# A hybrid decoder layer on one core: three raw weight buffers instead of two, seven slots of split weights instead of five, and the gates' row operations spread over more products

## The chip, the cores and the metric

The kernel runs on one core of one Trainium2 chip. The metric is the device time of one execution in microseconds (us). The time before is 2606.9 us, the median of three runs (2606.17 to 2619.28).

## The reference, cut to what matters

One layer is applied to 2048 prompt tokens and to 8 x 4 sample tokens, with D = 1024 and a feed-forward width of 2816, all in float32.

```
a = rmsnorm(x, g_mix);  u = a @ w_in            # q, k, v, gates, o, B, C, h
C_t = f_t C_{t-1} + i_t k_t v_t^T               # mLSTM, chunkwise, 4 heads
h = o * headnorm(q^T C / max(|q.n|, 1));  y = B * conv3(C * h)
x += concat(h, y) @ w_out
x += (silu(f @ w_gate) * (f @ w_up)) @ w_down   # f = rmsnorm(x, g_ffn)
x += sigmoid(x @ w_pg) * rmsnorm(p @ w_ple, g_ple)
y = rmsnorm(x, g_final)
```

The gates' rows are scalars for each head and token: log forget gates are summed within a chunk (a scan), a running maximum is taken (a second scan), and differences of these rows are exponentiated.

## The kernel before, in words

The tokens go through in three groups ("supers") 0, 1 and 2 of 704, 704 and 672 tokens, and each super goes through the whole layer. A product of TensorE is 12 matmuls of 128x128 weights with half a super's tokens (352 or 336 columns): a float32 product is made of three fp32r ones, high*high, high*low and low*high (`three`, L606). A pair of 256 output columns is computed by seven such products instead of eight (Strassen's scheme, P1 to P7), so sums of weight quarters (S1 to S4) are needed as well as the quarters themselves.

**The way of a weight.** SP loads raw float32 weights of a pair into one of the two buffers wraw (`raw`, L1071; raw r waits until raw r-2 is used up). DVE makes the four sums of a pair (L1771 S1, L1779 S2, L1783 S3, L1787 S4), 128x512 elements each; S3 and S4 overwrite parts of the raw buffer. ACT rounds a quarter or sum to its high part (L1294), and POOL subtracts to get the low part (L2688). Both parts of one entry lie in a slot of the ring wring (5 slots); entry e takes the slot of entry e-5, once TensorE's product with that is done (L1280). In super 0 SP writes the split sums to memory (weight_parts, L1088). In supers 1 and 2 ACT's queue loads them back into the ring (L1286) instead of DVE, ACT and POOL making them again; only A12 and A22 are then split anew. Each wait on a kept or loaded part is on one of six semaphores in turn.

**The order** is written out by hand: every engine walks through the same list of products and calls its `ahead()` once a product. ACT and POOL thereby prepare the entry four products ahead of TensorE; DVE makes its sum five ahead. These distances are set by the calls before the loop (four on ACT and POOL, `AHEAD + 1` on DVE, L2587), by the calls inside the first pair of a super (`Plain.aheads`, L99: at four of the eight products), and by two calls behind it. Because an engine is in order, whatever a call waits for also holds up the eviction that stands behind it.

**DVE** also combines the products out of PSUM: in the later pairs it reads P6 (L1851, which frees the bank that TensorE's P7 needs), P7 (L1858, L1824), P2, P4 and P3 (L1827, L1829); in the first pairs and those with four banks L1840, L1847, L1849, L1824. Two "duos" (w_out 0 and 1; w_gate 0 and w_up 0) interleave the products of two pairs, so that they need two raw buffers at once; ahead of each, DVE makes the operands (differences of activations and their low parts, L1797, L2027 to L2035), with L1908 reading P6. In the feed-forward stage DVE also makes the low part of the hidden layer behind each up pair (L2427, two of 128x704).

**The gates** are computed behind the products numbered s = 8 to 28 of a super: DVE makes masks at s = 8, logs at 11, both scans at 13 (L2078, L2079), the sample's scans (super 2 only) and all differences at 15 (L2101 to L2112), and the parts at 17 (L2118 to L2120).

SP's loop goes by raw r: it issues raw r, then what is due there (reloads of x at r = 13 and 14, next tiles at 51 to 53), then keeps the parts of raw r-1.

Of the kernel before, what the change touches and what calls it, by code (L numbers as in the profile page):

```python
# [7 lines left out]
F32 = mybir.dt.float32  # L8
# [26 lines left out]
RING = 5  # L35
AHEAD = 4
# [62 lines left out]
BY_TOKENS = Plain(("a", "b", "P2", "P4", "c", "d", "P3", "P5"), (0, 1, 2, 6), (0, 5, 6, 7))  # L99
# [67 lines left out]
def build(nc, x_prompt, x_sample, p_prompt, p_sample, state_C, state_n, state_m, state_conv, g_mix, w_in,  # L167
# [37 lines left out]
    wraw = [at(f"wraw{p}", [P, 2048], F32, w0 + p * 8192) for p in range(2)]  # L205
    spare_raw = at("spare_raw", [P, 2048], F32, w0 + 20480 + RING * 4096 + 5632)
# [5 lines left out]

    mix0 = w0 + 20480 + RING * 4096
    expE = at("expE", [P, NH, P], F32, mix0)
# [73 lines left out]
    y_roots = keep("y_roots", [P, 3])  # L288
    assert cursor[0] <= nc.sbuf_usable_end, (cursor[0], nc.sbuf_usable_end)
# [29 lines left out]
    n_sums, n_prepared, n_landed = [0], [0], [0, 0]  # L319
# [3 lines left out]
    def add_raw(pieces):  # L323

        r = len(raws)
        raws.append(pieces)
        end[r] = 0
        n_landed[r % 2] += 16 * len(pieces)
        raw_landed.append(n_landed[r % 2])
        return r, wraw[r % 2]  # L330
# [176 lines left out]
    with ExitStack() as ctx:  # L507
# [7 lines left out]
        landed = [sem("landed_even"), sem("landed_odd")]  # L515
        parts_kept, parts_loaded = [sem(f"parts_kept{j}") for j in range(6)], [sem(f"parts_loaded{j}") for j in range(6)]
# [49 lines left out]
        def _(pe):  # L566
# [26 lines left out]
            def entry_ready(e):  # L593
                w = entries[e]
                if w.prepared:
                    pe.wait_ge(lo_done, w.prepared)
                else:
                    pe.wait_ge(parts_loaded[w.loads % 6], 16 * ((w.loads + 5) // 6))
# [469 lines left out]
        def _(sp):  # L1068
            n_raw = [0]

            def raw():  # L1071

                r = n_raw[0]
                n_raw[0] += 1
                if r >= len(raws):
                    return
                if r >= 2:
                    sp.wait_ge(lo_done, raw_end[r - 2])
                for where, src in raws[r]:
                    sp.dma_start(wraw[r % 2][:, where].rearrange("p (k n) -> p k n", k=src.shape[1]), src)\  # L1080
                        .then_inc(landed[r % 2], 16)

            def keep_parts(which, names=None):

                for e, w in enumerate(entries):
                    if w.raw in which and w.kept and (names is None or names(w)):
                        sp.wait_ge(lo_done, w.prepared)
                        sp.dma_start(weight_parts[w.kept - 1], wring[e % RING][:, :].bitcast(F32))\  # L1088
                            .then_inc(parts_kept[w.kept % 6], 16)
# [172 lines left out]
        def _(act):  # L1262
# [8 lines left out]
            def one_ahead():  # L1271
# [6 lines left out]
                if e >= RING:  # L1278
                    if entries[e - RING].spare is None:
                        act.wait_ge(prod, entry_end[e - RING])  # L1280
                    before = entries[e - RING].kept
                    if before:
                        act.wait_ge(parts_kept[before % 6], 16 * ((before + 5) // 6))
                if w.loaded:
                    act.wait_ge(parts_kept[w.loaded % 6], 16 * ((w.loaded + 5) // 6))
                    act.dma_start(wring[e % RING][:, :].bitcast(F32), weight_parts[w.loaded - 1])\  # L1286
                        .then_inc(parts_loaded[w.loads % 6], 16)
                    return
                if w.first:
                    act.wait_ge(landed[w.raw % 2], raw_landed[w.raw])  # L1290
# [438 lines left out]
        def _(dve):  # L1729
# [31 lines left out]
            def one_ahead():  # L1761
# [5 lines left out]
                for name, r, v, where, turn, first, second in sums_at.get(e, ()):  # L1767
                    if name == "S1":
                        dve.wait_ge(landed[r % 2], raw_landed[r])
# [305 lines left out]

            def gate_scans(q):
                T, TP, n = q.T, q.TP, q.nch
                link(nc.vector.tensor_tensor_scan(B[0:NH, 0:T], W[0:NH, 0:T], LF[0:NH, 0:T], 0.0, mul, add))  # L2078
# [19 lines left out]
            def gate_weights(q):  # L2098
                T, TP = q.T, q.TP
                dve.wait_ge(parts_clear, NTILE * (q.n + 1))  # L2100
                link(nc.vector.tensor_tensor(R1[0:NH, 0:T], B[0:NH, 0:T], M[0:NH, 0:T], sub))  # L2101
                link(nc.vector.tensor_tensor(CS[0:NH, 0:T], G[0:NH, 0:T], B[0:NH, 0:T], sub))
                whole = TP // P * P
# [153 lines left out]
            def in_after(q):  # L2257
                def after(s):
# [660 lines left out]
```

## Time and profile before

| | us |
|---|---|
| median of three runs | 2606.9 |
| lowest and highest | 2606.17, 2619.28 |
| span of the profiled execution | 2611.0 |
| TensorE (PE) busy | 2487.7 |
| VectorE (DVE) busy | 1491.2 |
| ScalarE (ACT) busy | 906.9 |
| GpSimd (POOL) busy | 1050.4 |

The span runs from the first to the last instruction of one profiled execution. Its own time outside the profile is not given; the span lies 4.1 us over the median of the runs. "Idle before" and a bracket such as `[6.14 <-DVE u L1858]` give how long the engine stood idle before the instruction and what ended that. PEclk is the granted clock of TensorE: 1.00 is 2.4 GHz and 0.50 is 1.2 GHz.

### The profile page before, as it was taken

To read this page: it belongs to the slowest core of one execution; us is meant where nothing else is said; L and a number is where in the kernel's file an instruction comes from. 1 tells how busy PE (TensorE), PEld (TensorE's weight loads), DVE (VectorE), ACT (ScalarE), POOL (GpSimd) and SP (SyncE) were. 2 spreads that over 40 slices of the span, in tenths; PEclk is the share of its full clock that TensorE was granted. 3 is DMA by queue.
4 is the path that set the end of the run, shared out by engine and by line. 5 is a ranking of instruction groups with operands and counts; after the bars stand their busy time and mean duration, and the time that the engine had idled before them with its cause. 6 is when DMAs were issued, how large, how long until landed. Compare 5 with 4: busy or idle time off the path is not lost.

```text
span 2611.0 us, 41191 instructions
## 1 busy us (share of the span) xinstructions
PE 2487.7 (95%) x15829; PEld 2430.8 (93%) x15829; DVE 1491.2 (57%) x2287; ACT 906.9 (35%) x1688; POOL 1050.4 (40%) x864
## 2 busy tenths in 40 slices
PE   8898888999999999999999999999999999999998
PEld 7898788999999998999999999998899999999997
DVE  7667887665555683466643333468357664333355
ACT  5344453343334543334322121354134432212133
POOL 5666655576666342222332122333223232312233
PEclk8999899999999999999999999999999999999999
DMA  5656635576566746575556545575557555565545
GB/s 187 211 176 227 219 134 186 185 275 225 207 229 226 234 147 205 162 236 178 193 167 202 170 150 174 178 235 180 175 172 243 184 191 170 194 201 162 170 145 172
DMA packets 285046, 501.04 MB, mean 192 GB/s; under 512 B 18427, under 2 KB 182612, under 8 KB 284342
## 3 DMA queue, kind: packets, MB, share of 16 engines
q1 hardware_dynamic: 212182, 273.59, 31.1%
q10 hardware_dynamic: 72672, 224.82, 26.3%
q8 instruction: 129, 2.11, 0.3%
q14 instruction: 63, 0.52, 0.1%
HBM read 374.70 MB, written 123.65 MB: 191 GB/s over the span
## 4 chain that ended last, share of the span: by engine, by line
PE 72%; DVE 8%; DMA 4%; issue 3%; POOL 2%; ACT 1%; DVEq 0%; POOLq 0%; ACTq 0%; SPq 0%
PE bank L608 23%; PE bank L610 22%; PE bank L609 22%; DMA wring<-weight_parts 2%; POOL wring L2688 1%; DVE qlo L1797 1%; DMA xs<-x_prompt 1%; PE bank L732 1%; DVE ess L2410 1%; PE bank L743 1%; DMA wraw<-w_gate 0%; PE bank L797 0%; PE bank L803 0%; DVE wraw L1787 0%; DMA y_prompt<-y_rows 0%
## 5 line engine op out<-in xcount | busy, mean ns | idle before, releaser
L2688 POOL TENSOR_TENSOR wring<-wraw,wring 128x512 fp32r<-128x512 f32 x531 | 777.1, 1471 | 1214.9 <-ACT wring L1294 1210.5
L608 PE MATMUL bank<-qhi,wring 128*128 128x352 f32 (+1 forms) x3588 | 1172.9, 327 | 74.8 <-DVE u L1908 14.4
L610 PE MATMUL bank<-qhi,wring 128*128 128x352 f32 (+1 forms) x3588 | 1157.5, 323 | 0.0
L609 PE MATMUL bank<-qlo,wring 128*128 128x352 f32 (+1 forms) x3588 | 1155.6, 322 | 0.0
L608 PEld LDWEIGHTS bank<-qhi,wring 128*128 128x128 f32 x3588 | 683.6, 191 | 97.9 <-issue 84.6
L609 PEld LDWEIGHTS bank<-qlo,wring 128*128 128x128 f32 x3588 | 683.4, 190 | 0.0
L610 PEld LDWEIGHTS bank<-qhi,wring 128*128 128x128 f32 x3588 | 681.4, 190 | 0.0
L1294 ACT ACTIVATE wring<-wraw 128x512 fp32r<-128x512 f32 x531 | 331.3, 628 | 721.0 <-PE bank L610 553.5
L608 PE MATMUL bank<-hid,wring 128*128 128x352 f32 (+1 forms) x1056 | 340.6, 323 | 12.5 <-DVE wide L2493 7.4
L610 PE MATMUL bank<-hid,wring 128*128 128x352 f32 (+1 forms) x1056 | 339.3, 321 | 0.0
L609 PE MATMUL bank<-hid,wring 128*128 128x352 f32 (+1 forms) x1056 | 338.3, 320 | 0.0
L2493 DVE TENSOR_TENSOR wide<-wide,bank 128x352 f32<-128x352 f32 (+1 forms) x288 | 147.9, 514 | 293.9 <-PE bank L610 293.9
L608 PEld LDWEIGHTS bank<-hid,wring 128*128 128x128 f32 x1056 | 199.5, 189 | 16.6 <-issue 13.0
L609 PEld LDWEIGHTS bank<-hid,wring 128*128 128x128 f32 x1056 | 200.3, 190 | 0.0
L610 PEld LDWEIGHTS bank<-hid,wring 128*128 128x128 f32 x1056 | 199.3, 189 | 0.0
L1858 DVE TENSOR_TENSOR u<-t,bank 128x352 f32<-128x352 f32 (+1 forms) x84 | 43.1, 514 | 188.9 <-PE bank L610 188.8
L2688 POOL TENSOR_TENSOR wring<-s,wring 128x512 fp32r<-128x512 f32 x74 | 111.2, 1514 | 63.0 <-ACT wring L1294 62.5
L1851 DVE TENSOR_TENSOR u<-t,bank 128x352 f32<-128x352 f32 (+1 forms) x87 | 44.5, 511 | 134.3 <-PE bank L610 105.7
L1576 ACT ACTIVATE hid<-sl 128x704 fp32r<-128x704 f32 (+3 forms) x69 | 52.1, 754 | 188.3 <-DVE sl L1829 180.4
L2427 DVE TENSOR_TENSOR hid<-sl,hid 128x704 fp32r<-128x704 f32 (+3 forms) x69 | 101.7, 1486 | 10.0 <-ACT hid L1576 8.6
L1323 ACT ACTIVATE t<-bank 128x352 f32<-128x352 f32 (+1 forms) x123 | 56.3, 457 | 136.0 <-PE bank L610 136.0
L1294 ACT ACTIVATE wring<-s 128x512 fp32r<-128x512 f32 x74 | 45.7, 628 | 93.1 <-PE bank L610 49.9
(321 smaller groups left out, 2440.4 us busy)
## 6 DMA issues: line engine op xcount, KB each, us to landing
wring<-weight_parts ACTq DMA_DIRECT2D x418, 512.0 KB, 4.5
weight_parts<-wring SPq DMA_DIRECT2D x201, 512.0 KB, 4.0
wraw<-w_down SPq DMA_DIRECT2D x33, 1024.0 KB, 7.0
wraw<-w_in SPq DMA_DIRECT2D x14, 1024.0 KB, 7.0
wraw<-w_gate SPq DMA_DIRECT2D x11, 1024.0 KB, 6.1
wraw<-w_up SPq DMA_DIRECT2D x11, 1024.0 KB, 5.9
wraw<-w_in SPq DMA_DIRECT2D x44, 256.0 KB, 4.8
wraw<-w_gate SPq DMA_DIRECT2D x44, 256.0 KB, 4.1
```

What stands on the lines that cost most here:

```text
L608: nc.tensor.matmul(o, hi, mh, start=begins, stop=False, skip_group_check=True)
L609: nc.tensor.matmul(o, hi, ml, start=False, stop=False, skip_group_check=True)
L610: return nc.tensor.matmul(o, lo, mh, start=False, stop=ends, skip_group_check=True)
L732: last = nc.tensor.transpose(bank[bk][0:n, c * P:(c + 1) * P], q.X[:, m * 4 + c, t0:t0 + n], ident[:, :])
L1294: nc.scalar.activation(whi[e % RING][:, :].rearrange("p (k n) -> p k n", k=k), w.src, ACT.Copy).then_inc(hi_done, 1)
L1323: nc.scalar.activation(t1[n % 2][:, 0:q.N], bank[a][:, 0:q.N], ACT.Copy).then_inc(free[a], 1)
L1576: nc.scalar.activation(hid[:, 0, x, blk], sl[:, c, blk], ACT.Copy).then_inc(h_hi, 1)
L1851: nc.vector.tensor_tensor(w2, t, c, add).then_inc(fc, 1)
L1858: nc.vector.tensor_tensor(w3, w2 if first else t, d, add).then_inc(fd, 1)
L2427: nc.vector.tensor_tensor(hid[:, 1, x, blk], sl[:, c, blk], hid[:, 0, x, blk], sub).then_inc(h_lo, 1)
L2493: last = nc.vector.tensor_tensor(x, x, bank[bk][:, 0:q.N], add)
L2688: nc.gpsimd.tensor_tensor(wlo[e % RING][:, :].rearrange(v, k=k), w.src, whi[e % RING][:, :].rearrange(v, k=k), ALU.subtract).then_inc(lo_d ...
```

## The change

The raw buffers become three (`RAW_RING`), the ring gets seven slots (`RING`), and the semaphores of kept and loaded parts become eight. The room, 16 KB of each partition, is that of the scratch for transfers that GpSimd would issue; the kernel issues none there. Raw r now waits for raw r-3, and SP issues raw r+1 where it issued raw r. In the first pair of super 0 there are six calls of `ahead()` instead of four, and DVE has seven instead of five before the loop; ACT and POOL keep their four. The gates' first scan moves to s = 12, the sample's scans to 14, and the differences are split: R1 and CS at 15, the rest at 16. The second reload of x is waited for two corners earlier.

```diff
-RING = 5
-AHEAD = 4
+RING = 7
+N_PARTS = RING + 1
+RAW_RING = 3
+DMA_SCRATCH = 256
+AHEAD = 6
...
-BY_TOKENS = Plain(("a", "b", "P2", "P4", "c", "d", "P3", "P5"), (0, 1, 2, 6), (0, 5, 6, 7))
+BY_TOKENS = Plain(("a", "b", "P2", "P4", "c", "d", "P3", "P5"), (0, 1, 2, 6), (0, 3, 4, 5, 6, 7))
...
+    wraw = [at(f"wraw{p}", [P, 2048], F32, w0 + p * 8192) for p in range(2)]
+    wraw += [at(f"wraw{p}", [P, 2048], F32, cursor[0] + (p - 2) * 8192) for p in range(2, RAW_RING)]
+    cursor[0] += 8192 * (RAW_RING - 2)
...
-                if r >= 2:
-                    sp.wait_ge(lo_done, raw_end[r - 2])
+                if r >= RAW_RING:
+                    sp.wait_ge(lo_done, raw_end[r - RAW_RING])
...
-                    if (q.n, r) not in ((0, 0), (0, 1)):
+                    if (q.n, r) != (0, 0):
                         raw()
...
+            def gate_sums(q):
+                T = q.T
+                link(nc.vector.tensor_tensor_scan(B[0:NH, 0:T], W[0:NH, 0:T], LF[0:NH, 0:T], 0.0, mul, add))
...
+            def gate_differences(q):
+                T = q.T
                 dve.wait_ge(parts_clear, NTILE * (q.n + 1))
                 link(nc.vector.tensor_tensor(R1[0:NH, 0:T], B[0:NH, 0:T], M[0:NH, 0:T], sub))
                 link(nc.vector.tensor_tensor(CS[0:NH, 0:T], G[0:NH, 0:T], B[0:NH, 0:T], sub))
...
+                    if s == 12:
+                        gate_sums(q)
                     if s == 13:
                         gate_scans(q)
+                    if s == 14 and q.sample:
+                        sample_scans(q)
                     if s == 15:
-                        if q.sample:
-                            sample_scans(q)
+                        gate_differences(q)
+                    if s == 16:
                         gate_weights(q)
...
-                    if (c, b) == (0, 0) and i in (0, 2):
-                        dve.wait_ge(reload0 if i == 0 else reload1, 16 * (q.n + 1))
+                    if (i, c, b) == (0, 0, 0):
+                        dve.wait_ge(reload0, 16 * (q.n + 1))
+                    if (i, c, b) == (2, 1, 1):
+                        dve.wait_ge(reload1, 16 * (q.n + 1))
...
-    nc = bacc.Bacc("TRN2", target_bir_lowering=False, num_devices=1)
+    nc = bacc.Bacc("TRN2", target_bir_lowering=False, num_devices=1, dynamic_dma_scratch_size=DMA_SCRATCH)
```

## Rows read from the trace of the kernel before

**Rows 1.** The page of the profiled execution: span, busy time, granted clock.

```profile
span 2611.0 us, 41191 instructions
...
PE 2487.7 (95%) x15829; PEld 2430.8 (93%) x15829; DVE 1491.2 (57%) x2287; ACT 906.9 (35%) x1688; POOL 1050.4 (40%) x864
...
PEclk8999899999999999999999999999999999999999
```

**Rows 2.** Waits of PE: what it waited for, us in total, times, longest.

```profile
PE bank L608 <- DVE u L1908: 14.4, 3, 8.8
PE bank L608 <- DVE u L1851: 13.9, 10, 3.7
...
PE bank L608 <- DMA wring<-weight_parts: 6.1, 8, 2.7
...
PE bank L608 <- POOL wring L2688: 2.8, 2, 2.4
```

**Rows 3.** Busy time by stretch: length, PE, PEld, DVE, ACT, POOL, PEclk, DMA.

```profile
34.00:91.00 57.00, 49.66 (x272) 48.12 (x273) 54.48 (x56) 26.86 (x42) 39.65 (x25) 0.89 0.47 167
243.00:292.00 49.00, 30.51 (x173) 28.68 (x173) 41.86 (x39) 21.03 (x31) 31.26 (x17) 0.87 0.57 209
349.00:410.00 61.00, 47.04 (x271) 45.04 (x270) 55.56 (x55) 30.46 (x47) 33.38 (x21) 0.94 0.37 138
500.00:600.00 100.00, 97.22 (x607) 96.70 (x607) 55.69 (x77) 33.41 (x57) 63.45 (x44) 1.00 0.61 216
1160.30:1163.60 3.30, 3.30 (x14) 3.30 (x13) 3.30 (x2) 1.38 (x1) 1.11 (x1) 0.50 0.36 84
```

**Rows 4.** PE in order of time, the waits it ends.

```profile
258.95 0.63 PE L608 MATMUL bank<-qhi,wring 128*128 128x352 f32 x1 [6.14 <-DVE u L1858]
...
291.93 0.63 PE L608 MATMUL bank<-qhi,wring 128*128 128x352 f32 x1 [8.82 <-DVE u L1908]
...
86.44 0.63 PE L608 MATMUL bank<-qhi,wring 128*128 128x352 f32 x1 [6.63 <-DVE wide L1824]
```

**Rows 5.** DVE and SP in order of time around the first duo.

```profile
257.68 0.69 DVE L1771 TENSOR_TENSOR s<-wraw 128x512 f32<-128x512 f32 x1 [5.34 <-DMA wraw<-w_out]
...
251.25 0.43 SPq L1080 DMA_DIRECT2D wraw<-w_out  x1
```

**Rows 6.** DVE in order of time before and in the second duo.

```profile
349.31 2.05 DVE L2378 SCALAR_TENSOR_TENSOR R<-wide,gains,bank 128x352 f32<-128x352 f32 x4 [3.50 <-PE bank L743]
...
356.75 1.79 DVE L1779 TENSOR_TENSOR s<-s,wraw 128x512 f32<-128x512 f32 x1
...
367.02 0.68 DVE L1779 TENSOR_TENSOR s<-s,wraw 128x512 f32<-128x512 f32 x1
...
371.79 1.28 DVE L1783 TENSOR_TENSOR wraw<-wraw 128x512 f32<-128x512 f32 x2
```

**Rows 7.** DVE: groups of instructions, the weight sums: busy, mean ns, idle before.

```profile
L1787 DVE TENSOR_TENSOR wraw<-wraw,s 128x512 f32<-128x512 f32 x37 | 39.6, 1069 | 0.3 <-DVE plo L2347 0.2
```

**Rows 8.** DVE in order of time, a sum with POOL idle.

```profile
84.11 0.69 DVE L1783 TENSOR_TENSOR wraw<-wraw 128x512 f32<-128x512 f32 x1
```

**Rows 9.** DVE and PE at one boundary of pairs in the feed-forward stage.

```profile
571.96 3.88 DVE L2427 TENSOR_TENSOR hid<-sl,hid 128x704 fp32r<-128x704 f32 x2
575.76 1.75 DVE L1787 TENSOR_TENSOR wraw<-wraw,s 128x512 f32<-128x512 f32 x1
...
578.09 0.40 PE L608 MATMUL bank<-qhi,wring 128*128 128x352 f32 x1 [2.23 <-DVE u L1851]
```

**Rows 10.** Supers 1 and 2: three waits of PE, one issue of loads.

```profile
1158.91 0.43 PE L608 MATMUL bank<-qhi,wring 128*128 128x352 f32 x1 [2.67 <-DMA wring<-weight_parts]
...
1150.53 0.82 ACTq L1286 DMA_DIRECT2D wring<-weight_parts  x2
...
1860.66 0.42 PE L608 MATMUL bank<-qhi,wring 128*128 128x336 f32 x1 [2.35 <-POOL wring L2688]
...
1824.40 0.39 PE L608 MATMUL bank<-qhi,wring 128*128 128x336 f32 x1 [1.62 <-DVE wide L1824]
```

More of the change, by code:

```diff
@@ L204, in build @@
     w0 = R0 + 8 * SLOT
-    wraw = [at(f"wraw{p}", [P, 2048], F32, w0 + p * 8192) for p in range(2)]
-    spare_raw = at("spare_raw", [P, 2048], F32, w0 + 20480 + RING * 4096 + 5632)
     s1 = at("s1", [P, 4, P], F32, w0 + 16384)
@@ L213, in build @@
     mix0 = w0 + 20480 + RING * 4096
+    spare_raw = at("spare_raw", [P, 2048], F32, mix0 + 5632)
     expE = at("expE", [P, NH, P], F32, mix0)
@@ L318, in build @@
     end, duo_raws = {}, []
-    n_sums, n_prepared, n_landed = [0], [0], [0, 0]
+    n_sums, n_prepared, n_landed = [0], [0], [0] * RAW_RING
     n_kept, n_loads, kept_as = [0], [0], {}
@@ L327, in add_raw @@
         end[r] = 0
-        n_landed[r % 2] += 16 * len(pieces)
-        raw_landed.append(n_landed[r % 2])
-        return r, wraw[r % 2]
+        n_landed[r % RAW_RING] += 16 * len(pieces)
+        raw_landed.append(n_landed[r % RAW_RING])
+        return r, wraw[r % RAW_RING]
     def add_entry(r, src, total=0, first=False):
@@ L514, in build @@
             sem(n) for n in ("gains_in", "consts_in", "consts_made", "eps_made"))
-        landed = [sem("landed_even"), sem("landed_odd")]
-        parts_kept, parts_loaded = [sem(f"parts_kept{j}") for j in range(6)], [sem(f"parts_loaded{j}") for j in range(6)]
+        landed = [sem(f"landed{p}") for p in range(RAW_RING)]
+        parts_kept = [sem(f"parts_kept{j}") for j in range(N_PARTS)]
+        parts_loaded = [sem(f"parts_loaded{j}") for j in range(N_PARTS)]
         sums, hi_done, lo_done, prod = sem("sums"), sem("hi_done"), sem("lo_done"), sem("prod")
@@ L597, in entry_ready @@
                 else:
-                    pe.wait_ge(parts_loaded[w.loads % 6], 16 * ((w.loads + 5) // 6))
+                    pe.wait_ge(parts_loaded[w.loads % N_PARTS], 16 * -(-w.loads // N_PARTS))
             def operand_ready(q, st, i):
@@ L1076, in raw @@
                     return
-                if r >= 2:
-                    sp.wait_ge(lo_done, raw_end[r - 2])
+                if r >= RAW_RING:
+                    sp.wait_ge(lo_done, raw_end[r - RAW_RING])
                 for where, src in raws[r]:
-                    sp.dma_start(wraw[r % 2][:, where].rearrange("p (k n) -> p k n", k=src.shape[1]), src)\
-                        .then_inc(landed[r % 2], 16)
+                    sp.dma_start(wraw[r % RAW_RING][:, where].rearrange("p (k n) -> p k n", k=src.shape[1]), src)\
+                        .then_inc(landed[r % RAW_RING], 16)
             def keep_parts(which, names=None):
@@ L1282, in one_ahead @@
                     if before:
-                        act.wait_ge(parts_kept[before % 6], 16 * ((before + 5) // 6))
+                        act.wait_ge(parts_kept[before % N_PARTS], 16 * -(-before // N_PARTS))
                 if w.loaded:
-                    act.wait_ge(parts_kept[w.loaded % 6], 16 * ((w.loaded + 5) // 6))
+                    act.wait_ge(parts_kept[w.loaded % N_PARTS], 16 * -(-w.loaded // N_PARTS))
                     act.dma_start(wring[e % RING][:, :].bitcast(F32), weight_parts[w.loaded - 1])\
-                        .then_inc(parts_loaded[w.loads % 6], 16)
+                        .then_inc(parts_loaded[w.loads % N_PARTS], 16)
                     return
                 if w.first:
-                    act.wait_ge(landed[w.raw % 2], raw_landed[w.raw])
+                    act.wait_ge(landed[w.raw % RAW_RING], raw_landed[w.raw])
                 if w.total:
@@ L2102, in gate_weights @@
                 link(nc.vector.tensor_tensor(CS[0:NH, 0:T], G[0:NH, 0:T], B[0:NH, 0:T], sub))
+            def gate_weights(q):
+                T, TP = q.T, q.TP
                 whole = TP // P * P
```

9 lines of the change are left out of this document (3 added, 6 removed).

## The prediction

> **What bounds the kernel now.** Read the page first: PE is busy for 2487.7 of 2611.0 us, DVE for 1491.2 [rows 1]. No matmul is added or removed, so the 123.3 us in which PE stands idle, and the time it loses at half clock, are all that can be won; the other way, every new wait of PE is paid in full. Then the waits of PE [rows 2]: the long ones are for banks that DVE frees late (L1908 and L1851, and L1824 in [rows 4]), and few are for a weight (DMA 6.1 us, POOL 2.8). Third, the table of stretches [rows 3]: from 500 to 600 us PE is busy 97.22 of 100 us with DVE at 55.69. From 243 to 292 us, around the first duo, PE is busy for only 30.51 of 49 us while DVE is busy for 41.86; from 349 to 410, around the second, 47.04 of 61 while DVE has 55.56. So super 0 is bound by DVE at its duos and by PE elsewhere, and a stall must be priced by DVE's work there, not by its share of 57%.
>
> **Two unit prices.** A product is 12 matmuls; 607 matmuls in 100 us [rows 3] make it about 1.95 us. After a long wait the granted clock falls: behind the wait that ended at 1158.91 a stretch of 3.3 us has PEclk 0.50 (1.2 GHz) and 14 matmuls where 20 were due [rows 3, 10], so such a fall costs 6 x 0.16 = 1.0 us more.
>
> **How far ahead the change lets each engine go.** ACT and POOL have four calls before the loop, then six instead of four in the first pair, then two: by the second pair they are six products ahead instead of four. DVE has seven, six and two: 15 calls where it had 11, so its sums run nine ahead instead of five, three before ACT wants them. In supers 1 and 2 DVE has no sums, and ACT's loads are issued two products (3.9 us) sooner.
>
> **Part 1, loads and splits in supers 1 and 2: -8.8 us.** PE waited 2.67 us for a load that ACT had issued at 1150.53, behind a wait of its own [rows 10]; seven smaller ones bring such waits to 6.1 us [rows 2]. I take 5.5. The largest is under 3.9, so two products more cover all. One fall of the clock goes with them (1.0). The low part that PE waited 2.35 us for at 1860.66, while POOL built the sample's masked queries [rows 10], is covered in the same way. Bounds: 0 (loads only queue behind each other) and -10. I take -8.8, since every row is shorter than the lead gained.
>
> **Part 2, third raw buffer at the first duo: -6.8 us.** The second raw of the duo was issued at 251.25, only when the last entry of the pair two before was split; DVE waited 5.34 us for it, and PE 6.14 behind DVE [rows 4, 5]. With three buffers it is issued one pair (7 x 1.95 = 13.7 us) earlier and is there. But this does not give 6.14 plus the 8.82 that follow [rows 4]: DVE is the bound from there to the end of the duo. Its busy 41.86 us lose about one sum (nine sums lie in the stretch now; eight after the shift by four entries): -1.07 [rows 7]. A new wait comes: a duo builds S2 in the buffer of S1, so DVE, now at S2 five products before the duo, waits until POOL has split S1, which ACT may start only when PE has freed the slot at that product. I price it at one rounding and one subtraction, about 2 us, half of it hidden: +1. 49 - 41.86 = 7.1 us of DVE idleness become about 1.4; with the 1.07 off, the stretch shortens by 5.7 + 1.1 = 6.8 us. Bounds: 0, if other work fills in for the wait removed, and -15 (both waits of rows 4).
>
> **Part 3, the second duo: -2 us.** Both S2 and both S3, 1.79 + 0.68 + 1.28 = 3.75 us, stand in DVE's chain between 349.31 and PE's wait now [rows 6]; nine ahead, they move before the residual's mean. But there they stand in front of that mean, and S2 waits for POOL: the mean comes about 2.6 us later (a split of 1.3 and the sums, less what PE's own work on the column sums hides), and DVE, which had 3.50 us idle before 349.31, starts the norm later. Two sums of the next pair move in, and the four before the wait at L1851 behind the duo move out. Net -1, and another 1 us from raws that no longer land late. Bounds -8 and +4.
>
> **Part 4, boundaries in super 0's feed-forward stage: +3 us.** Behind each up pair DVE does two L2427 (3.88 us), then S4 (1.75), then L1851, for which PE waits 2.23 us in this case [rows 9]. Nine ahead, S3 stands where S4 stood, and an S2 lands one product earlier. DVE works through these rows without a gap; ahead of them it still waits for PE for some 0.3 us, by my estimate. A sum takes 0.69 us with POOL idle [rows 8] and 1.75 beside POOL [rows 9]. So each of nine such boundaries gets 0.4 us more at the low price and 1.5 at the high; I take 0.4 for eight of them, since the waits there are mostly 0.6 us and the sums in those the short ones. Bounds 0 and +14.
>
> **Part 5, the start and the gates of super 0: +2.3 us.** From 34 to 91 us DVE is busy for 54.48 of 57 us [rows 3], and the wait of PE that ends at 86.44 is 6.63 us [rows 4]. Spreading the gates moves the last row operations from s = 15 to 16, but the bank PE waits for is freed at s = 17, behind both. The total that DVE must do before it is the same plus one sum (1.07), and three sums now stand before the operands of pair 1, so part of the wait appears there, as a second one with its own fall of the clock (1.0). Bounds -9 (the wait and its fall go) and +6.
>
> **Part 6, gates of super 2: -1.6 us.** DVE's eight small scans of the sample move to s = 14, ahead of a wait for POOL, and PE's 1.62 us at 1824.40 [rows 10] go. In super 1, nothing.
>
> At nothing: the earlier issue by SP (its queue waits for POOL nearly all the time, and raw r+1 waits for work that ended one pair ago; it stands before the reloads, the embeddings and the tiles of x, so it is held by them no more than before); one more 1 MB transfer in flight, with DMA engines busy at 0.57 to 0.61 [rows 3]; the two moved reload waits, whose data SP asks for well before either place. If SP did stall, the duo's raws would be late as now.
>
> **Sum.** -8.8 - 6.8 - 2 + 3 + 2.3 - 1.6 = -13.9 us, against the profiled span of 2611.0; that lies 4.1 us over the median of the runs, so I take the difference to the median: 2606.9 - 13.9 = 2593.0. A measurement of this kernel can tell 0.5%, 13.0 us, from no change, so the forecast stands on that line.
>
> **Rivals.**
> *The duos give nothing (0.22).* DVE is the bound there, and what it does not wait for the raw it waits for POOL's split of S1. For: it was continuously busy behind the wait. Against: 7.1 us of idleness are in the row [rows 3]. Parts 2 and 3 go: 2593.0 + 8.8 = 2601.8.
>
> *Decoupling wins more (0.20).* With sums ready three products before ACT, ACT's evictions and POOL's splits are no longer held up by a late DVE, and the 8.82 us wait falls by another 6, the second duo's by 4, the gates' by 2, with a fall of the clock: -13. For: ACT stood behind DVE in both. Against: DVE's own work is not less. 2580.
>
> *Sums block at the boundaries, slower (0.14).* The same sum takes 0.69 us alone and 1.75 beside a subtraction of POOL [rows 8, 9]. If each S2 moved to a boundary falls on such a subtraction, nine boundaries and five of the input projection get 1.5 us each, and each wait grows past what makes the clock fall (1.0 more): 14 x 2.5 = 35 instead of 3, so 2593.0 + 32 = 2625. It passes 2620 once the mean new cost is 2.1 us. Against: DVE has 44 of 100 us free between the boundaries. The Trainium skill ("SBUF — State Buffer", section "Who interferes with whom") says that a VectorE instruction with two SBUF inputs and a GpSimd instruction that reads SBUF exclude each other: whichever issues second blocks until the first has finished. By that rule the moved sum pays a whole subtraction each time POOL is first, which is this rival; the rows' 0.69 and 1.75 agree with it, but not with its happening every time, since the mean of 37 is 1.07 [rows 7].
>
> *The gates' spread works in super 0 (0.02)*, against part 5: 6.63 and its fall go, 2583.
>
> **Chances.** The forecast has 0.42, with a range of its own of 2585 to 2601: half of it lies below 2593.9. Faster by over 0.5%: 0.23 + 0.20 + 0.02 + 0.01 = 0.46; within: 0.19 + 0.20 = 0.39; slower: 0.15, with what I have not seen. The range 2576 to 2613 leaves out the slow rival and the far end of the fast one.
>
> **What would show it.** Right: no wait for L1771 on a DMA at the duo and under 13 us of PE idle from 243 to 292; no waits for weight_parts over 0.5 us; 1.62 gone in super 2; a larger wait before 60 us and a smaller one at 86. Waits for L1851 from 450 to 810 that stay within 0.5 us of now show part 4 small; waits of over 2 us there, with PEclk 0.50 behind them, show the slow rival. The prediction is wrong if PE's idle total falls by less than 6 us or by over 25.

## The result and the profile after

The changed kernel takes 2625.9 us (median of 10 runs, 2618.7 to 2633.1) where the kernel before, on the same chip, takes 2610.5 (10 runs): ratio 1.0052, 95% interval 1.0040 to 1.0063. It is slower by 0.5%. The forecast was faster by 0.5%. Ratios here and below leave out three executions in the series of e5 to e8, two of the kernel before and one of e7, that took 4568 to 8536 us (e7's median of 2588.0 counts it, and is 2587.4 without).

The page of the changed kernel:

```profile
span 2625.1 us, 41144 instructions
...
PE 2493.5 (95%) x15829; PEld 2436.8 (93%) x15829; DVE 1482.7 (56%) x2287; ACT 911.3 (35%) x1688; POOL 1043.1 (40%) x864
...
PEclk8999899999999999999999999999999999999999
```

Against [rows 1] the span is 14.1 us longer, of which PE's busy time has 5.8 (the same matmuls, more of them at the low clock: the mean granted clock is 0.980 where it was 0.984) and PE's idle time the other 8.3, where the prediction called itself wrong if the idle time fell by less than 6. DVE's busy time has fallen. So it is not more work; work stands in front of PE that did not before. The waits of PE, whole span (what it waited for: us in total, times, longest):

```profile
PE bank L614 <- DVE u L1914: 19.1, 7, 9.9
PE bank L614 <- DVE u L1857: 16.8, 8, 3.7
...
PE bank L614 <- DVE t L1833: 8.3, 3, 5.9
...
PE bank L614 <- DVE u L1864: 3.5, 2, 2.9
PE bank L614 <- ACT wide L1362: 2.8, 1, 2.8
```

Lines have moved by 6 in the pair code: L1914, L1857, L1864 and L1833 are L1908, L1851, L1858 and L1827 of [rows 2]. No row for weight_parts or for wring is left: the loads and splits of supers 1 and 2 are in time, as forecast. What grew by over 1 us is all waits for DVE, except for two on ACT: the eviction L1362, which is new, and L1559 (3.4 to 4.5).

**Where the time went.** Take five of the lines with which DVE combines a product out of PSUM: L1846, L1855, L1864, L1914 and L2511, which adds the down products (before: L1840, L1849, L1858, L1908, L2493). Their 435 instructions stand in the same order in every kernel, so the end of the nth of them, called mark n, shows the same progress. The first line has its time in the kernel before, the others the difference to it, in us, each from the profiled execution.

| mark | 4 | 13 | 14 | 20 | 23 | 122 | 142 | 286 | 435 |
|---|---|---|---|---|---|---|---|---|---|
| before | 85.7 | 235.7 | 258.8 | 333.1 | 412.2 | 822.5 | 900.6 | 1730.7 | 2587.7 |
| changed | +2.6 | +9.3 | +11.9 | +11.3 | +7.5 | +22.0 | +20.2 | +17.6 | +13.5 |
| e1 (DVE seven ahead) | +1.5 | +6.4 | +1.3 | +0.1 | +0.1 | +11.1 | +9.4 | +6.5 | +2.3 |
| e2 (slots, old lookahead) | -2.8 | -2.5 | -7.1 | -9.1 | -10.3 | -10.8 | -13.0 | -14.5 | -20.4 |
| e3 (third raw alone) | -0.1 | -0.1 | -4.4 | -5.7 | -6.3 | -7.5 | -5.8 | -6.3 | -2.0 |
| e5 (e2 with five slots) | -3.2 | -3.2 | -7.6 | -9.7 | -11.0 | -11.3 | -10.0 | -9.5 | -5.1 |
| e7 (five and six ahead) | +1.2 | +5.6 | +2.5 | -0.2 | -4.2 | -4.5 | -7.3 | -15.7 | -26.3 |
| e8 (three and four ahead) | -0.3 | -1.1 | -3.8 | -4.1 | -11.3 | -7.9 | -4.5 | +11.1 | +23.3 |
| e9 (sums cut) | -0.3 | +3.6 | +7.2 | +5.8 | +2.1 | -5.4 | -7.3 | -10.4 | -15.7 |
| e12 (sums placed) | +0.5 | +4.2 | +6.7 | +6.0 | +0.4 | -4.0 | -5.9 | -7.8 | -12.4 |
| e13 (duos' sums moved) | +0.7 | +4.4 | +2.8 | +3.8 | +0.4 | +14.6 | +12.9 | +12.6 | +8.4 |
| e14 (e12 and e13) | +3.3 | +7.0 | +5.4 | +6.5 | -1.3 | -6.4 | -9.0 | -12.4 | -16.2 |
| e15 (late five, placed) | -3.8 | -3.9 | -8.5 | -10.1 | -11.9 | -20.6 | -23.0 | -31.0 | -42.6 |

Each line is one execution, and a part of it is chance. Up to mark 13 the changed kernel, e9, e12, e13 and e14 run the same work in the same order, and yet they stand at -0.3 to +3.3 at mark 4 and at +3.6 to +9.3 at mark 13. So up to 6 us between two lines there mean nothing by themselves. The difference over a later stretch repeats better: from mark 13 to 14 the changed kernel and e12 lose 2.6 and 2.5 us, e13 and e14 win 1.6 each; from mark 142 to the end, where these five kernels are the same again, they win 4.5 to 8.4.

The changed kernel loses 9.3 us before the first duo (the four others 3.6 to 7.0), gains a little at the second, loses 14.5 us in the feed-forward stage of super 0 (7.5 to 22.0, marks 23 to 122), and wins 6.7 us in supers 1 and 2 (behind mark 142).

**One boundary.** DVE of the changed kernel at the last boundary of the stage, in order of time (start, length, line, what it works on); then POOL, and the matmul of PE that waited:

```profile
819.19 0.68 DVE L1785 TENSOR_TENSOR s<-s,wraw 128x512 f32<-128x512 f32 x1
819.79 0.51 DVE L1833 TENSOR_TENSOR u<-u,bank 128x352 f32<-128x352 f32 x1
820.33 0.53 DVE L1835 TENSOR_TENSOR sl<-sl,u 128x352 f32<-128x352 f32 x1
820.77 3.87 DVE L2445 TENSOR_TENSOR hid<-sl,hid 128x704 fp32r<-128x704 f32 x2
824.57 1.74 DVE L1789 TENSOR_TENSOR wraw<-wraw 128x512 f32<-128x512 f32 x1
826.24 0.51 DVE L1857 TENSOR_TENSOR u<-t,bank 128x352 f32<-128x352 f32 x1
```

```profile
823.86 3.58 POOL L2706 TENSOR_TENSOR wring<-s,wring 128x512 fp32r<-128x512 f32 x2
```

```profile
826.89 0.40 PE L614 MATMUL bank<-qhi,wring 128*128 128x352 f32 x1 [3.68 <-DVE u L1857]
```

S2 (L1785, 0.68 us) stands ahead of the last combination of the old pair, S3 (L1789, 1.74, beside POOL) ahead of the first of the new one, and DVE has no gap between them, so PE waits 3.68 us. S1 (L1777) has gone just before, 1.34 us from 816.38. It is much the same at the five boundaries where PE waits for L1857: S2 takes 0.68 or 0.69 us at every one, S3 1.74 to 1.77 at four of them and 0.68 at the fifth, where the wait is 1.32. The wait brings the clock down as well. Stretches of the changed kernel (length, PE, PEld, DVE, ACT, POOL, PEclk, DMA): the one behind this wait, and the whole feed-forward stage:

```profile
826.90:830.20 3.30, 3.30 (x14) 3.30 (x15) 0.28 (x1) 0.24 (x1) 0.55 (x1) 0.66 0.96 336
425.00:850.00 425.00, 405.05 (x2483) 401.81 (x2482) 249.92 (x345) 149.72 (x254) 263.75 (x187) 0.98 0.61 217
```

**The first duo.** The raw matrix is there, but PE waits 5.88 us (until 257.94) for a combination (L1833), 2.90 (until 270.85) for L1864 and 9.90 (until 303.14) for L1914, where before it waited 6.14 and 8.82 [rows 4]. DVE, then POOL, of the changed kernel:

```profile
251.19 5.45 DVE L2245 TENSOR_TENSOR wide<-wide,wide 128x1152 f32<-128x1152 f32 x1
256.67 0.69 DVE L1777 TENSOR_TENSOR s<-wraw 128x512 f32<-128x512 f32 x1
257.28 0.51 DVE L1833 TENSOR_TENSOR t<-t,bank 128x352 f32<-128x352 f32 x1
...
266.20 0.69 DVE L1785 TENSOR_TENSOR s<-s,wraw 128x512 f32<-128x512 f32 x1 [3.94 <-POOL wring L2706]
266.81 1.62 DVE L1803 TENSOR_TENSOR qlo<-wide,qhi 128x1408 fp32r<-128x1408 f32 x1
269.58 0.69 DVE L1785 TENSOR_TENSOR s<-s,wraw 128x512 f32<-128x512 f32 x1 [1.15 <-POOL wring L2706]
270.19 0.51 DVE L1864 TENSOR_TENSOR u<-t,bank 128x352 f32<-128x352 f32 x1
```

```profile
249.48 1.00 POOL L2807 TENSOR_TENSOR sm<-sm,neg_half 64x4 f32<-64x4 f32 x1 [3.02 <-DVE sm L2184]
250.46 4.96 POOL L2706 TENSOR_TENSOR wring<-wraw,wring 128x512 fp32r<-128x512 f32 x4
```

Two things: S2 waits 3.94 and 1.15 us for POOL's split of S1 with a combination queued behind it, and one elementwise product (L2245, both inputs in SBUF) takes 5.45 us while POOL, which had stood behind its own wait, does four subtractions in one go.

### The profile page after: what moved, and what is told of

It is laid out like the page before. It is cut to its first block, busy times and chain, and to the rows that moved or that the text cites. A ratio compares the mean times of both kernels' runs of the same rounds, so it can differ in the third digit from the quotient of the medians.

```text
span 2625.1 us, 41144 instructions
## 1 busy us (share of the span) xinstructions
PE 2493.5 (95%) x15829; PEld 2436.8 (93%) x15829; DVE 1482.7 (56%) x2287; ACT 911.3 (35%) x1688; POOL 1043.1 (40%) x864
## 4 chain that ended last, share of the span: by engine, by line
PE 72%; DVE 7%; issue 3%; POOL 3%; ACT 1%; DMA 0%; DVEq 0%; ACTq 0%; POOLq 0%
PE bank L614 23%; PE bank L616 22%; PE bank L615 22%; POOL wring L2706 2%; DVE qlo L1803 1%; DVE hid L2445 1%; DVE sl L1835 1%; PE bank L738 0%; PE bank L749 0%; DVE s L1777 0%; PE bank L803 0%; PE bank L727 0%; PE bank L777 0%; DVE ess L2428 0%; PE bank L809 0%
## 5 line engine op out<-in xcount | busy, mean ns | idle before, releaser
L2511 DVE TENSOR_TENSOR wide<-wide,bank 128x352 f32<-128x352 f32 (+1 forms) x288 | 147.5, 514 | 282.6 <-PE bank L616 282.1
L1864 DVE TENSOR_TENSOR u<-t,bank 128x352 f32<-128x352 f32 (+1 forms) x84 | 43.2, 514 | 225.3 <-PE bank L616 225.2
L1857 DVE TENSOR_TENSOR u<-t,bank 128x352 f32<-128x352 f32 (+1 forms) x87 | 44.5, 511 | 131.0 <-PE bank L616 104.0
L2445 DVE TENSOR_TENSOR hid<-sl,hid 128x704 fp32r<-128x704 f32 (+3 forms) x69 | 76.1, 1111 | 27.0 <-ACT hid L1582 26.5
L1833 DVE TENSOR_TENSOR u<-u,bank 128x352 f32<-128x352 f32 (+1 forms) x96 | 49.3, 514 | 38.5 <-PE bank L616 34.3
```

What stands on the lines that cost most here:

```text
L1833: nc.vector.tensor_tensor(tmp, acc, psum, add).then_inc(own_free, 1)
L1857: nc.vector.tensor_tensor(w2, t, c, add).then_inc(fc, 1)
L1864: nc.vector.tensor_tensor(w3, w2 if first else t, d, add).then_inc(fd, 1)
L2445: nc.vector.tensor_tensor(hid[:, 1, x, blk], sl[:, c, blk], hid[:, 0, x, blk], sub).then_inc(h_lo, 1)
L2511: last = nc.vector.tensor_tensor(x, x, bank[bk][:, 0:q.N], add)
```

## The experiments

Theory A says: DVE's deeper lookahead moves the weight sums to the products of a pair where DVE has no room, and makes S2 in a duo wait for POOL. Rivals: the depth on ACT and POOL or the seven slots (B; later G, depth itself), the third raw buffer (C), the gates (D). Ratios are to the kernel before in the same series. "L" is how many entries ahead DVE's sums run from the second pair on; L moves S1, S2, S3 and S4 (entries 0, 1, 3, 6) to other products of the pair before.

**e1: DVE's sums seven ahead.**

```diff
-            for e in range(AHEAD + 1):
+            for e in range(AHEAD - 1):
```

> The changed kernel with the sums on DVE made seven entries ahead, not nine (two calls fewer before the loop); ACT and POOL keep six. Theory A (the nine entries are the cause: in super 0 the sums S1, S2, S4 of the next pair fall on the last three products of a pair, in front of the sum over PSUM that TensorE waits for, and in the duos S2 waits for POOL's subtraction of S1): 2610 us, between 2605 and 2616, ratio to before 0.998 to 1.002, the 20 us lost by the end of super 0 shrink to under 6, and no DVE wait for lo of S1 in the duos. Rival B (six entries on ACT and POOL, or seven slots, are the cause), rival C (the third raw buffer with SP's new order) and rival D (the gates spread) all leave it at 2622 to 2626.

Measured: 2612.7 us, ratio 1.0002 (0.9993 to 1.0012). The two calls cost 13 us (0.0050 of 2611). That is theory A's value. DVE waits for no split of POOL at the first duo any more, but for 2.55 us at the second. Theory A's "under 6 us lost by the end of super 0" did not come (+9.4): the feed-forward stage still loses 11 us (+0.1 to +11.1).

**e2: the slots without the lookahead.**

```diff
-AHEAD = 6
+AHEAD = 4
-BY_TOKENS = Plain(..., (0, 3, 4, 5, 6, 7))
+BY_TOKENS = Plain(..., (0, 5, 6, 7))
```

> The changed kernel with the lookahead of before on all three engines (four entries on ACT and POOL, five on DVE); seven slots, three raw buffers and the spread gates stay. Theory A and rival B (it is lookahead): 2604 to 2612 us, ratio 0.998 to 1.001; the wait for weight parts in supers 1 and 2 (6.1 us in all before) is back. Rival C or D: 2620 or more.

Measured: 2593.3 us, ratio 0.9931 (0.9918 to 0.9944): lookahead is the cause, but the value lies some 11 us below both theories' range. The rest of the change is worth 18 us, and the lookahead takes 32 (0.0121 of 2611). Of the weights' waits only one of any size is left in super 1 (2.8 us).

**e3: the third raw buffer and SP's order alone.** RING 5, RAW_RING 3, everything else as before.

> The kernel before with the third raw buffer and SP's new order of loads alone (five slots, the lookahead and gates of before). My prediction's part 2 gave this 6.8 us at the first duo and some of part 3's 2: 2601 to 2604. Theory A as it stands now says that the duo was late by DVE too: raw matrices land in time (the 5.34 us wait of DVE for w_out goes), and the time is 2604 to 2611. Rival C: 2618 or more, super 0 longer by over 10 us.

Measured: 2608.6 us, ratio 0.9992 (0.9981 to 1.0004). The total is not clear of no change. In the trace it wins 4.3 us at the first duo (-0.1 to -4.4), 6.3 by the end of the second, and gives 3.8 back in supers 1 and 2 (-5.8 to -2.0), which is no more than chance can make. PE's waits from 235 to 300 us in e3, where [rows 4] has 6.14:

```profile
PE bank L614 <- DVE u L1914: 8.8, 1, 8.8
PE bank L614 <- DVE u L1864: 1.8, 1, 1.8
PE bank L614 <- DVE u L1833: 1.7, 1, 1.7
PE bank L614 <- DVE t L1833: 1.6, 1, 1.6
```

**e4: the spread gates alone.** The kernel before with the gate functions and their places of the change.

> The kernel before with the gates' row operations spread over products 12 to 16 alone. Theory A: 2608 to 2611, ratio 0.999 to 1.000 (the two waits of 84 to 87 us, 6.6 us in all before, become 5 or stay). Rival D: 2616 or more.

Measured: 2609.6 us, ratio 0.9999 (0.9987 to 1.0010). The wait near 86 us is 6.22 (before 6.63), the one of super 2 1.25 (before 1.62): nothing to speak of either way.

**e5: e2 with five slots.** `RING = 5`.

> Five slots and the lookahead of before, with the third raw buffer and the spread gates: the kernel of e2 with its two more slots taken away. Theory A (the two more slots are what made e2 20 us faster than before: with the lookahead kept, each high part may be written two products before it used to be): 2605 to 2611 us, ratio to before 0.998 to 1.000, and e2's head start of 2.5 us in the first 30 us is gone. Rival F (raw buffer and gates each give nothing alone but gain together): 2593 to 2600.

Measured: 2606.4 us, ratio 0.9978 (0.9968 to 0.9988). So two slots more are worth 12 us (0.9978 less 0.9931). Not in the first 30 us, as I had read it: the trace of e5 has that head start too, by chance. It is won behind super 0: from mark 142 to the end e2 wins 7.4 us and e5 loses 4.9. PE's waits behind 900 us in e5:

```profile
PE bank L614 <- DMA wring<-weight_parts: 6.6, 8, 1.9
PE bank L614 <- POOL wring L2706: 2.6, 1, 2.6
```

**e6: e2 with six slots.** `RING = 6`.

> The kernel of e2 with six slots in place of seven (lookahead of before, three raw buffers, spread gates). Theory A: most of the gain is in the first slot more, as it gives a whole product of room: 2593 to 2600 us. Rival: both slots are needed, 2600 to 2606.

Measured: 2598.4 us, ratio 0.9942 (0.9927 to 0.9957): the sixth slot is worth 9 us, the seventh 3, though the last is within the intervals.

**e7: one entry more on each engine.** Five calls in the first pair, DVE five before the loop.

> The kernel of e2 with one entry more of lookahead on each engine (five on ACT and POOL, six on DVE; seven slots). Theory A in its form by place (what counts is on which products of a pair the sums fall: with six, S1 on the second, S2 on the third, S3 on the fifth, S4 on the first, so still one sum alone in the last three): 2591 to 2598 us. Rival G (depth itself costs: every entry more at the start of a super puts copies and sums in front of work that TensorE waits for): 2598 to 2606, with a wait of over 1 us for ACT near 45 us.

Measured: 2588.0 us, ratio 0.9905 (0.9887 to 0.9923), below both ranges. Super 0 keeps its length in the feed-forward stage (-4.2 to -4.5) but is 8 us later than e2 by the first duo, 4 of them at mark 4 already (the wait for L1833 is 3.4 us there, 1.35 in e2); supers 1 and 2 win 19.0 us where e2 wins 7.4. So depth does cost at the start and the duo, as rival G says, and pays for it later.

**e8: one entry less.**

```diff
-BY_TOKENS = Plain(..., (0, 5, 6, 7))
+BY_TOKENS = Plain(..., (0, 6, 7))
```

> The kernel of e2 with one entry less on each engine (three on ACT and POOL, four on DVE; seven slots). By place: with four, S1 falls on the fourth product, S2 on the fifth, S3 on the last, so three sums lie in front of the boundary: 2603 to 2615 us, the feed-forward stage of super 0 longer by 5 to 12 us. Rival G (depth costs): 2585 to 2592. A third way: the weights come too late for TensorE at stage changes, waits for POOL's wring appear and the time is over 2600 for that.

Measured: 2630.9 us, ratio 1.0070 (1.0055 to 1.0085), above theory A's range. It is the third way: of the 36 us between e2 and e8, 44 in their traces, the feed-forward stage has only 4 (+3.4 against -0.5), and supers 1 and 2 have 35 (-4.5 to +23.3 against -13.0 to -20.4), where the weights come late. The waits of PE, whole span:

```profile
PE bank L614 <- DMA wring<-weight_parts: 20.5, 12, 4.6
PE bank L614 <- POOL wring L2706: 16.0, 12, 3.2
```

**e9: the changed kernel with the sums of the feed-forward weights of super 0 cut to 4 columns** (the rest of those sums is left out).

```diff
+                    w = slice(0, 1) if duo_raws[1][1] < r < RAWS else slice(0, P)
-  nc.vector.tensor_tensor(first[:, :, :], v["A21"], v["A22"], add)
+  nc.vector.tensor_tensor(first[:, :, w], v["A21"][:, :, w], v["A22"][:, :, w], add)
...                                              # S2, S3 and S4 in the same way
```

> The changed kernel with DVE's sums S1 to S4 of the feed-forward weights of super 0 (all pairs behind the duo) cut from 512 to 4 columns each; their order, waits and signals stay. Left out: the sums over the rest of those weights. It asks what the sums themselves cost at the boundaries. Theory A (two or three sums, each 0.7 us alone and 1.5 to 1.8 beside POOL's subtraction, lie in front of the sum over PSUM): the waits for L1857 between 468 and 823 us (1.3 to 3.7 us each) fall under 0.5, the 14 us lost in the feed-forward stage go: 2608 to 2613 us. Rival G (six entries deep on ACT and POOL, whose copies and hidden's highs come late): the waits stay, 2621 or more.

Measured: 2603.7 us, ratio 0.9961 (0.9946 to 0.9977), 24 us less than the changed kernel and below theory A's range. The waits for L1857 from 425 to 850 us fall from 12.8 us to 2.1 with ACT and POOL as deep as they were, so rival G is out for them.

**e10: the same cut in e2.**

> The same cut (sums of 4 columns in the feed-forward stage of super 0) in the kernel of e2, as the measure of what sums cost where they fall well. Theory A: its boundaries wait 0.57 us ten times, so 3 to 6 us go: 2587 to 2591. If DVE's load as such (and not where the sums fall) is what costs, it gains as much as e9, 14 us: 2579.

Measured: 2580.4 us, ratio 0.9877 (0.9860 to 0.9893), 14 us less than e2. So both readings hold a part: DVE's work in that stage costs 14 us where the sums stand well, and 10 more where they stand badly. I had expected 3 to 6.

**e11: e2 in super 0, five and six ahead from super 1 on.**

```diff
+BY_WEIGHTS_1 = Plain(..., (0, 2, 4, 5, 6))   # super 1; super 2 keeps (0, 2, 4, 6)
```

> The kernel of e2 in super 0 (four and five entries ahead), and from the start of super 1 one more on each engine (five and six). Theory A: e7 lost 6 us against e2 by the end of super 0 (at the start and at the first duo) and won 12 in supers 1 and 2; the two add up, so 2579 to 2584 us, faster than every kernel so far. Rival: what e7 won in supers 1 and 2 came from its state at the end of super 0, then 2588 to 2594.

Measured: 2583.7 us, ratio 0.9884 (0.9867 to 0.9900), within theory A's range: supers 1 and 2 win 18.2 us by its trace (-11.1 at mark 142 to -29.3), as in e7.

**e12: the changed kernel, sums of gate and up pairs placed by hand.** The calls of the engines and the work are the same. But a sum that is made later is also made less far ahead of its use: here S1 five entries ahead, S2 six, S3 seven and S4 nine, where all four had nine.

```diff
-for j, n in zip((0, 4, 6, 10) if two else (0, 1, 3, 6), turns):
+for j, n in zip((0, 4, 6, 10) if two else (4, 4, 5, 6) if of[0][0] in ("gate", "up") else (0, 1, 3, 6), turns):
```

> The changed kernel as it is (six entries ahead on ACT and POOL, nine calls on DVE), with the sums of the gate and up pairs alone placed by hand: their places in a pair's entries go from 0, 1, 3, 6 to 4, 4, 5, 6, so that S1 and S2 are made on the third product of the pair before, S3 on the fourth, S4 on the fifth, and none on the last two or the first two. Theory A (place, not depth or work): the boundary waits of 1.3 to 3.7 us for L1857 go below 1.1 us, the 14.5 us that the changed kernel loses between 412 and 822 us shrink to under 3: 2611 to 2616 us, ratio to before about 1.000. Rival (the depth of DVE's sums, or DVE's load, costs wherever they stand): 2621 or more.

Measured: 2602.9 us, ratio 0.9964 (0.9953 to 0.9976): 23 us less than the changed kernel for one table, as much as leaving the sums out (e9), and below the range that theory A had given. DVE and PE at the boundary shown above:

```profile
797.72 3.89 DVE L2445 TENSOR_TENSOR hid<-sl,hid 128x704 fp32r<-128x704 f32 x2
801.54 0.51 DVE L1857 TENSOR_TENSOR u<-t,bank 128x352 f32<-128x352 f32 x1
801.97 1.34 DVE L1777 TENSOR_TENSOR s<-wraw 128x512 f32<-128x512 f32 x1
803.44 0.69 DVE L1785 TENSOR_TENSOR s<-s,wraw 128x512 f32<-128x512 f32 x1
804.05 0.68 DVE L1789 TENSOR_TENSOR wraw<-wraw 128x512 f32<-128x512 f32 x1
```

```profile
802.19 0.40 PE L614 MATMUL bank<-qhi,wring 128*128 128x352 f32 x1 [0.20 <-DVE u L1857]
```

The sums stand behind L1857 now, where nobody waits for DVE. From mark 23 to mark 122, the same work in both, e12 needs 405.9 us, 6.2 of them with PE idle, and the changed kernel 424.8 with 20.1 idle. The stretch by time:

```profile
425.00:850.00 425.00, 421.95 (x2628) 419.34 (x2628) 256.99 (x364) 156.05 (x267) 275.19 (x190) 0.99 0.62 219
```

**e13: the changed kernel, sums of the duos moved.** `(0, 4, 6, 10)` becomes `(0, 6, 8, 10)`.

> The changed kernel with the duos' sums alone moved: places 0, 4, 6, 10 become 0, 6, 8, 10, so S2 is made when POOL has subtracted S1 (two products later), S3 two later as well. Theory A (in the duo DVE, nine entries ahead, reaches S2 before POOL, six ahead, has split S1, and stands 3.9 and 1.2 us with TensorE's sums behind it): the waits of 5.88 us near 252 and 2.90 near 268 fall to some 1.5 each, the loss of 2.6 us over the first duo becomes a gain as in e2: 2616 to 2621 us. Rival (the copies of ACT at the stage changes hold the duo up): 2624 or more.

Measured: 2620.2 us, ratio 1.0034 (1.0023 to 1.0046), 5 us less. DVE no longer waits for POOL:

```profile
257.19 1.62 DVE L1803 TENSOR_TENSOR qlo<-wide,qhi 128x1408 fp32r<-128x1408 f32 x1
261.09 0.52 DVE L1864 TENSOR_TENSOR u<-t,bank 128x352 f32<-128x352 f32 x1 [2.29 <-PE bank L616]
...
265.39 0.69 DVE L1785 TENSOR_TENSOR s<-s,wraw 128x512 f32<-128x512 f32 x1
```

From mark 13 to 14 a loss of 2.6 us turns into a gain of 1.6. But the wait of 5.88 us stays: I had put it down to S2, and it is L2245's 5.45 us, which this kernel has too. And a later wait of 3.34 us for L1833 appears, since the moved sums now stand in front of that, so that of the 4.2 us only 2.6 are left by mark 20.

**e14: both.**

> Both moves of e12 and e13 in the changed kernel. If the two causes are apart they add up: 2601 to 2611 us, ratio 0.996 to 0.999, which is where e1 and my prediction's sum would put a kernel whose lookahead costs nothing at the boundaries; the rest up to the 2593 of e2 is the start and the in stage (some 8 us by 235 us). If one hides the other: 2612 to 2618.

Measured: 2597.7 us, ratio 0.9947 (0.9933 to 0.9961), 27 us less than the changed kernel; e12 and e13 won 23 and 5. The two causes are apart and add up, within the intervals of some 3 us each. The time is 3 us below the range given.

**e15: e11 with placed sums.** `(0, 1, 3, 6)` becomes `(0, 1, 2, 3)` for gate and up pairs: third to sixth product of the pair before.

> The kernel of e11 (four and five entries ahead in super 0, five and six after) with the sums of the gate and up pairs placed by hand: 0, 1, 3, 6 become 0, 1, 2, 3 (third, fourth, fifth and sixth product of the pair before). e10 says that these sums cost 13 us at most in this arrangement. Theory A: the eight waits of 0.57 us go, 3 to 6 us are gained: 2577 to 2581 us. Rival: the sixth product (a sum there too) costs as much as the second did: 2582 to 2585.

Measured: 2572.9 us, ratio 0.9861 (0.9841 to 0.9881), 1.4% faster than the kernel before, the fastest of all, and 4 us below the range given. Its page:

```profile
span 2568.7 us, 41148 instructions
...
PE 2471.6 (96%) x15829; PEld 2417.2 (94%) x15829; DVE 1485.1 (58%) x2287; ACT 895.9 (35%) x1688; POOL 1054.1 (41%) x864
```

**The places, side by side.** PE's wait for L1857 from 425 to 850 us, and the products of a pair on which S1, S2, S3 and S4 of the next are made. The combination L1857 stands on the second product, behind the two L2445 of the seventh.

| kernel | L | S1, S2, S3, S4 on product | waits for L1857, us | ratio |
|---|---|---|---|---|
| changed | 9 | 6, 7, 2, 5 | 12.8 | 1.0052 |
| e1 | 7 | 1, 2, 4, 7 | 12.1 | 1.0002 |
| before | 5 | 3, 4, 6, 2 | 6.9 | 1 |
| e2 | 5 | 3, 4, 6, 2 | 6.3 | 0.9931 |
| e7 | 6 | 2, 3, 5, 1 | 5.9 | 0.9905 |
| e8 | 4 | 4, 5, 7, 3 | 8.2 | 1.0070 |
| e12 | 9 | 3, 3, 4, 5 | 0.7 | 0.9964 |
| e15 | 5 | 3, 4, 5, 6 | 0.5 | 0.9861 |

With three of the four sums on products 6, 7, 1 and 2 the waits are 12 to 13 us, with two 6 to 7, with none (e12) or one on the sixth (e15) under 1. e8, with one on the seventh, has 8.2, so the count alone is not the whole rule; why that one costs so much was not tried by itself.

Is it the place, or how far ahead of its use a sum is made? e12 changes both. e15 answers: its sums are made five to eight entries ahead (S1 and S2 five, S3 six, S4 eight), none less far than in e2 (five), with the same calls in super 0, and the waits fall from 6.3 us to 0.5. It is the place.

## Why the prediction was wrong

By the marks, measured against forecast: the changed kernel is 13.5 us later where 13.9 earlier was forecast, 27.4 us in all. The largest share, and the step that failed, is part 4; three smaller ones follow. The measured parts below are differences between two executions, with the chance told above.

- **Part 4, boundaries (+3 forecast, +14.5 measured).** This is the step that failed, by 11.5 us. The mechanism stood in the text (DVE goes through the rows ahead of L1851 without a gap, so one more sum there comes late), and so did the 1.75 us beside POOL; the size was off. I counted one moved sum at each boundary, at the low price of 0.4, and S1, with 1.34 us on product 6, not at all. Three of the four land on products 6, 7 and 2, and two of the waits pass 3.6 us, with the fall of the clock behind them. e12 shows it: the same work, placed otherwise, wins 23 us. Of the 14.5 us PE's idle time has 10.1: 5.9 for L1857 (12.8 less 6.9), 3.3 in four new waits of 0.82 for L2511, and 0.9 in the wait for L2511 at the stage's start (3.73; 2.81 before). The other 4.4 are PE's busy time, the low clock.
- **The slow rival** (0.14 in the text) named the right place and nearly the right time (ratio 1.0052 on 2606.9 is 2620.5, against its 2625), but that was in part luck. It had 14 sums S2 that each fall on a subtraction of POOL, at 2.5 us each. At the five boundaries where PE waits for L1857, S2 fell on none (0.68 or 0.69 us each time). S3 fell on one at four of them, at the 1.75 us that S4 has in [rows 9]. The loss was 2.9 us at each of the five (14.5 / 5), and what made it was how many sums stand in front of the combination.
- **Part 2, first duo (-6.8 forecast, +2.0 measured, marks 13 to 20).** The third raw buffer wins most of what was forecast when it comes alone (e3: 5.6 us between these marks), but in the changed kernel two costs of depth cover it. S2's wait for POOL was priced at +1 and is 3.94 and 1.15 us; e13, without it, wins 4.2 us by mark 14 and 2.6 by mark 20. L2245's 5.45 us was not in the text at all.
- **The in stage (nothing forecast, +6.7 measured, marks 4 to 13).** Only the slow rival named it. Some 3 us of it are chance: e9, e12, e13 and e14 run the same work there and lose 3.7 to 3.9. PE is idle as long in the changed kernel as in e12 (7.1 and 7.5 us); what differs is its busy time for the same 965 matmuls, with the granted clock at 0.95 against 0.98 (changed, then e12):

```profile
88.30:245.00 156.70, 149.65 (x965) 141.18 (x966) 97.99 (x174) 68.24 (x174) 93.63 (x87) 0.95 0.55 194
86.20:239.90 153.70, 146.19 (x965) 137.82 (x966) 98.62 (x175) 68.26 (x174) 93.67 (x87) 0.98 0.56 198
```

The other 3.7 us repeat: the waits that end at 159.7 for L1857 (2.87 us; 1.99 before) and at 233.0 for L1830 (2.41; not there before) stand in all five kernels with the same lengths. e7 and e1 lose 4 to 5 us there too, e2 nothing. It was not tested by itself which engine's depth does it.
- **Parts 1 and 6, supers 1 and 2 (-10.4 forecast, -6.7 measured).** The waits for loads and for POOL went, as written. Waits for L1914 came in their stead: 7.3 us behind 900 us, where the kernel before has 0.6. The reason given was half right: e2 wins 7.4 us there with no lookahead at all, from slots alone. With the calls of before, two slots more take the waits for loads behind 900 us from 6.6 (e5) to 2.8 us (e2), so ACT came to its loads early enough and was held by the slot they go into. That the slots have a worth of their own (12 us) stands nowhere in my parts, and it is the largest gain of the change. Part 6 gives nothing: the wait of 1.62 us is 1.25 in e4 and in the changed kernel.
- **Part 3 (-2 forecast, -3.8 measured, marks 20 to 23)** came out (e9 and e13 have -3.7 and -3.4 there). DVE waits 1.54 and 2.70 us for POOL's split of S1, as written, and the stretch is shorter all the same.
- **Part 5 (+2.3 forecast, +2.6 measured)** is open, and that the numbers agree is luck: at mark 4 the five kernels with the same work stand at -0.3 to +3.3. The wait near 86 us did shrink (6.63 to 5.01, and to 3.4 in e12) and others came before it, as written, but e4 shows that the gates' order alone does nothing (6.22). What is new is ACT's eviction L1362, for which PE waits 2.78 us until 48.0, behind copies moved ahead, and 4.48 in e12.

Why supers 1 and 2 run best five ahead (19.0 us in e7, 18.2 in e11; 4.5 to 8.4 in the five kernels with six, 7.4 in e2 with four) is open. Six has waits of up to 2.8 us for L1914 at the duos of supers 1 and 2 that five has not above 1.0; the cause of these was not tried either.

## What to carry to other kernels

A deeper lookahead in a loop whose work is laid out by hand is two changes: it adds slack, and it turns every helper's work round within the period. Write down on which step each helper instruction lands for the new depth, modulo the period, and keep them off the steps in front of what the bottleneck waits for; here one table of four numbers was worth 23 us, more than the two slots (12) or the third raw buffer (2 in e3, not clear of nothing). And test buffers and depth apart: slots of the ring gained 12 us with the depth left alone, and the depth took more than that back.

## What the runs showed of the hardware

The same DVE instruction with two inputs in SBUF (L2245, 128x1152 f32) took 1.76 us in e2, 3.01 in e1, 4.22 in e7 and 5.45 in the changed kernel and e13. It starts inside the first subtraction of a run of POOL, and the run is of one subtraction in e2, two in e1, three in e7 and four in the changed kernel. In every trace, of the kernel before and of all fifteen experiments too, it ends 1.22 us behind the last subtraction of that run: in the changed kernel it starts at 251.19, POOL's four last from 250.46 to 255.42, and it ends at 256.64. PE's wait for L1833, which stands behind it on DVE, grows with it: 1.35 us in e2, 2.25 in e1, 3.37 in e7 and 5.88 in the changed kernel. In e2:

```profile
238.51 1.76 DVE L2245 TENSOR_TENSOR wide<-wide,wide 128x1152 f32<-128x1152 f32 x1
240.30 0.69 DVE L1789 TENSOR_TENSOR wraw<-wraw 128x512 f32<-128x512 f32 x1
```

```profile
237.78 1.27 POOL L2706 TENSOR_TENSOR wring<-s,wring 128x512 fp32r<-128x512 f32 x1
241.81 4.55 POOL L2706 TENSOR_TENSOR wring<-wraw,wring 128x512 fp32r<-128x512 f32 x3 [2.77 <-ACT wring L1300]
```

The prediction cited the Trainium skill ("SBUF — State Buffer", section "Who interferes with whom"), by which the instruction that issues second waits until the first has finished. For a run of one (e2) the trace agrees. For longer runs it does not: in the changed kernel the DVE instruction was held over four, not one. Subtractions that stand ready behind each other can keep it out; but at 823.86, in a run of two, DVE's sum did get between them (it took 1.74 us in place of 0.69 and ended 0.55 us behind the first, and POOL's two took 3.58). When a run of POOL lets DVE in and when not was not tested by itself. A backlog is what makes such runs here: POOL had stood 3.02 us behind a wait for DVE while ACT went on making its copies, and each of the four was made before POOL came to it. The depth alone does not set how long the run is: it is one subtraction with ACT and POOL four entries ahead (e2), three with five (e7) and four with six (changed), but two with six in e1, where DVE's sums are less deep, and two with three in e8.
